# A second layout of the expert input's shift and scale: small products on TensorE, or a pass through DRAM

## What is computed

```python
mod = (jax.nn.silu(c) @ ada_w + ada_b)[:, None, :]
sh1, sc1, gt1, sh2, sc2, gt2 = jnp.split(mod, 6, axis=-1)
...
x = x + gt1 * (merged @ w_out)
h2 = rmsnorm(x, norm2_g) * (1.0 + sc2) + sh2
x = x + gt2 * hier_moe(h2, rg_w, rg_b, re_w, re_b, e_gate, e_up, e_down)
```

## Time and profile before

| | us |
|---|---|
| median of 3 runs | 2064.58 (2064.09 to 2065.99) |
| time of the profiled execution | 2064.39 |
| span of the profiled execution, first to last instruction | 2062.5 |
| PE busy in the span | 1926.4 |
| DVE busy | 1130.1 |
| ACT busy | 900.5 |

### The profile page before, as it was taken

How to read it: one execution, slowest core, us unless ns; L and a number is a source line. 1 busy time by engine, 2 the same in 40 slices (tenths; PEclk the granted TensorE clock), 3 DMA queues, 4 the chain that set the end, 5 groups by cost and what they waited for, 6 DMA issues and landing times.

```text
span 2062.5 us, 30821 instructions
## 1 busy us (share of the span) xinstructions
PE 1926.4 (93%) x12904; PEld 1493.4 (72%) x12904; DVE 1130.1 (55%) x1527; ACT 900.5 (44%) x1279; POOL 111.1 (5%) x91
## 2 busy tenths in 40 slices
PE   9999999999999876666699999999999999999998
PEld 7899988889984211111168888888888888988887
DVE  3778774577662110011146666756666766756666
ACT  4655455545352100000045556545455545675554
POOL 0244121001110000000000000000000000000000
PEclk9999999999999989898899999999999999999999
DMA  9654544678999999999986755544555555524552
GB/s 350 207 166 144 172 135 154 201 247 282 333 379 416 422 421 421 422 421 421 420 317 202 235 184 184 184 163 164 184 188 179 184 184 186 174 92 170 192 184 82
DMA packets 247505, 503.51 MB, mean 244 GB/s; under 512 B 12097, under 2 KB 166338, under 8 KB 223042
## 3 DMA queue, kind: packets, MB, share of 16 engines
q1 hardware_dynamic: 246464, 500.70, 67.5%
q10 hardware_dynamic: 898, 0.80, 0.1%
HBM read 500.07 MB, written 1.06 MB: 243 GB/s over the span
## 4 chain that ended last, share of the span: by engine, by line
PE 75%; DMA 12%; DVE 5%; SPq 3%; ACT 3%; issue 2%; POOL 0%; ACTq 0%; DVEq 0%
PE bank L600 14%; PE bank L602 14%; PE bank L601 14%; PE bank L661 13%; PE bank L663 7%; DMA m<-in_expert_w_up 5%; SPq L3298 3%; DMA m<-in_expert_w_down 3%; PE bank L1056 3%; DMA m<-in_expert_w_gate 2%; PE bank L1067 1%; PE bank L937 1%; DVE m L2225 1%; DMA m<-in_ffn_w_in 1%; ACT m L1532 1%
## 5 line engine op out<-in xcount | busy, mean ns | idle before, releaser
L2225 DVE TENSOR_TENSOR m<-m,m 128x1024 fp32r<-128x1024 f32 x505 | 623.0, 1248 | 281.2 <-ACT m L1532 279.0
L600 PE MATMUL bank<-m,m 128*128 128x256 f32 (+1 forms) x1960 | 662.3, 338 | 8.6 <-DVE m L2225 5.0
L602 PE MATMUL bank<-m,m 128*128 128x256 f32 (+1 forms) x1960 | 646.4, 330 | 0.0
L601 PE MATMUL bank<-m,m 128*128 128x256 f32 (+1 forms) x1960 | 646.3, 330 | 0.0
L1532 ACT ACTIVATE m<-m 128x1024 fp32r<-128x1024 f32 x505 | 523.7, 1054 | 219.7 <-PE bank L602 202.5
L661 PE MATMUL bank<-m,m 128*128 128x512 f32 x1248 | 439.8, 394 | 0.0
L600 PEld LDWEIGHTS bank<-m,m 128*128 128x128 f32 x1960 | 369.0, 188 | 58.6 <-DVE m L2225 11.5
L602 PEld LDWEIGHTS bank<-m,m 128*128 128x128 f32 x1960 | 369.1, 188 | 36.8
L601 PEld LDWEIGHTS bank<-m,m 128*128 128x128 f32 x1960 | 369.4, 188 | 35.4 <-issue 2.4
L663 PE MATMUL bank<-m,m 128*128 128x256 f32 x1248 | 353.0, 283 | 0.0
L661 PEld LDWEIGHTS bank<-m,m 128*128 128x128 f32 x1248 | 234.4, 188 | 53.7
(11 more groups left out here) (347 smaller groups left out, 1370.1 us busy)
## 6 DMA issues: line engine op xcount, KB each, us to landing
m<-in_ffn_w_in SPq DMA_DIRECT2D x88, 1024.0 KB, 5.1
m<-in_expert_w_up SPq DMA_DIRECT2D x64, 1024.0 KB, 26.4
m<-in_expert_w_gate SPq DMA_DIRECT2D x63, 1024.0 KB, 26.1
m<-in_w_in SPq DMA_DIRECT2D x60, 1024.0 KB, 5.2
m<-in_expert_w_down SPq DMA_DIRECT2D x60, 1024.0 KB, 26.1
m<-in_ffn_w_out SPq DMA_DIRECT2D x44, 1024.0 KB, 4.9
m<-in_ada_w SPq DMA_DIRECT2D x24, 1024.0 KB, 5.7
m<-in_a_w_in SPq DMA_DIRECT2D x16, 1024.0 KB, 5.3
```

The lines of the kernel that those rows point to most:

```text
L600: e.matmul(o, s[0], m[0], start=first, stop=False, skip_group_check=skip)
L601: e.matmul(o, s[0], m[1], start=False, stop=False, skip_group_check=skip)
L602: return e.matmul(o, s[1], m[0], start=False, stop=last, skip_group_check=skip)
L2225: inc(e.tensor_tensor(rv(fit(q.L, q.view.shape)), q.view, fit(q.H, q.view.shape), ALU.subtract), "l", skey(q, "L"))
```

## The change

The second set of products goes: PE no longer makes the `adap` sums, DVE no longer adds the bias to them, and `vp` shrinks to the gain `norm2_g` (one small load in place of three). Instead SP, in branch B step 1 behind the router's four small loads, writes the 16 finished columns of `cols` to the DRAM scratch, one number of 4 bytes at a time since neighbours on a partition lie 128 numbers apart in DRAM. In branch B step 2, behind the loads of that step's two products, SP waits for that write and reads the scratch back into `colp` in the other layout, 256 runs of 32 bytes.

```diff
-        vp, colp, g2p = tiny(24), tiny(16), tiny(8)
+        vp, colp, g2p = tiny(8), tiny(16), tiny(8)
...
                     full(ins, "ada", g)
-                    if g in (6, 7, 8, 9):
-                        b = take("s", "adap", g)
-                        half = 64 * (g % 2)
-                        for k in range(8):
-                            for r in (0, 32):
-                                ins = e.matmul(b[half + r:half + r + 32, 64 * k:64 * k + 4], acc[g][:, 8 * r + k:8 * r + 256:8],
-                                               K(C_ONE, 4), start=True, stop=True, skip_group_check=True)
-                        full(ins, "adap", g)
...
-                        if g in (6, 7, 8, 9):
-                            b = got("adap", g)
-                            w.wait_ge("vp")
-                            c, r = 8 * (kind - 3), slice(64 * half, 64 * half + 64)
-                            taken(e.tensor_tensor(colp[r, c:c + 8], b[r, 0:512:64], vp[r, c:c + 8], ALU.add), "adap", g,
-                                  also=[("colp", g)])
...
-                w.wait_ge("colp", 9)
-                inc(e.scalar_tensor_tensor(out=g2p, in0=colp[:, 8:16], scalar=1.0, in1=vp[:, 16:24], op0=ALU.add,
+                w.wait_ge("colp")
+                w.wait_ge("vp")
+                inc(e.scalar_tensor_tensor(out=g2p, in0=colp[:, 8:16], scalar=1.0, in1=vp, op0=ALU.add,
                                            op1=ALU.mult), "router", ("g2p",))
...
                     if name == "B" and i == 1:
                         w.wait_ge("full", ("ocT", 7))
                         router_in()
+                        w.wait_ge("aM")
+                        for g in range(6, 10):
+                            w.wait_ge("cols", g)
+                        then_inc(e.dma_start(bass.AP(tensor=scr, offset=0, ap=[[1, 128], [128, 16]]), cols[:, 16:32],
+                                             allow_slow_non_contiguous=True),
+                                 "scr_out", ("colq",), by=16)
+                    if name == "B" and i == 2:
+                        w.wait_ge("colq")
+                        in_rows = bass.AP(tensor=scr, offset=0, ap=[[8, 128], [1024, 2], [1, 8]])
+                        then_inc(e.dma_start(colp.rearrange("p (z k) -> p z k", z=2), in_rows), "skew_in", ("colp",), by=16)
...
-            for i, src in enumerate((a["ada_b"][0][3072:4096], a["ada_b"][0][4096:5120], a["norm2_g"][0])):
-                then_inc(e.dma_start(vp[:, 8 * i:8 * i + 8], src.rearrange("(p k) -> p k", k=8)), "vp_in", ("vp",), by=16)
+            then_inc(e.dma_start(vp, a["norm2_g"][0].rearrange("(p k) -> p k", k=8)), "vp_in", ("vp",), by=16)
```

## The result

The changed kernel takes **2068.49 us** (median of 20 runs, 2066.84 to 2070.26), the kernel before 2064.97 (20 runs beside them, 2063.78 to 2066.99). The ratio is 1.0017, with a 95% interval of 1.0011 to 1.0022: slower by 3.5 us, about 0.17%. The forecast was 2060.6 and the range ended at 2067.5. What came is near rival C, which had priced itself at 2068.1.

The account below looks back on a forecast made before the run. PE was taken to bound the product stages and to release the experts' DMA-bound stream. From the median 2064.58 us, -3.92 for PE and 0 for the rest, with the write's 3.0 us hidden, gave 2060.6; range 2059.4 to 2067.5.

Parts of the forecast that it names:

- rival C: DMA queue before branch C's first load: writes cost more than reads, 12.6 us, PE stalls 7.4, 2068.1 us; chance 0.15.
- The removed products: PE, groups 6 to 9: four places lose 0.98 us each, 3.92 us in all, passed on to the experts' stream.
- Rival D: From 505 to the experts: the DMA stream bounds, an earlier PE only waits longer, time near 2064.4; chance 0.04.
- The price of the write: SP's queue ahead of branch C's weight loads: 1.4 us issue plus 1.6 us packets, 3.0 us delay.
- the dear end of 7.0: Same write priced at full packets, 5.6 + 1.4 us: a PE stall of 1.8 us, gain shrinks to 2.1.
- The cover: Branch C's first weight load, landing at 508.98, may land as late as 514.1: 5.2 us of delay hidden.
- The sum: Whole kernel: -3.92 us for PE, 0 for the rest, giving 2060.6 us, 0.19% faster.
- estimate of 25.6 us for the write: The write, from the skill page's 0.2 us HBM latency: 128 accesses in turn on each engine, time near 2082.
- SP's wait and the read: SP, branch B step 2: write through at 505.8, 3.7 us left until 509.45, read 0.2 us; DVE does not wait.
- Rival E: Two early loads or freed banks give something, at most 2.08 us at the start: 2058.6 to 2059.8; chance 0.08.
- What would show it: Changed profile: no PE weight wait from 500 to 540 and `w_out` 3.9 us earlier confirm; a stall near 512 refutes.
- B: Branch C: the write costs 5.2 to 9.1 us, PE stalls, part of the gain lost, 2061.4 to 2064.5; chance 0.13.

Follow-up runs that it names:

- experiment 1: The changed kernel without the write to DRAM and the wait for it, the read kept: 2060.81 us, ratio 0.998 to the kernel before.
- (3): The changed kernel with the block transposed on PE and written as 16 rows of 512 B, whole computation: 2060.85 us, ratio 0.9981.
- twin read (2): The changed kernel with a read of the same 2048 4-byte pieces in the write's place, no second DMA: 2061.15 us, ratio 0.9983.
- 8: The changed kernel with the 2048 numbers written 64 bytes apart, whole computation: 2063.45 us, ratio 0.9991.
- 5: The changed kernel with 256 bytes between the written numbers, read back in two DMAs, whole computation: 2062.52 us, ratio 0.9991.
- (6): The changed kernel with only the eight shift columns written, 1024 pieces in place of 2048: 2066.72 us, ratio 1.0009.
- (4): The changed kernel with 20 idle 128 x 128 products on PE ahead of branch C's first wait: 2066.12 us, ratio 1.0005.

## Why the prediction was wrong, point by point

- **The removed products: right.** 4 x 0.98 = 3.92 us forecast. Branch B starts 4.23 us earlier (0.21 of it is there before the first of the four places, 386.60 - 386.39), and without the write (1) or with cheap rows (3) the kernel is 4.2 us faster, so the gain is passed on to the end, as claimed. Rival D falls.
- **The price of the write: the step that failed.** "I lean to the low half, since the nearest rows in size and place are the router's small packets." The rows were reads, and the twin read (2) shows that they price a read well: about 1 us. The write delays the load behind it by 10.9 us instead of the 3.0 taken, and the dear end of 7.0 did not hold it either. A price per packet was the wrong form: with a distance of 64 or 256 bytes as many writes cost 3.4 and 2.5 us (8, 5), and half as many neighbours cost 8.3 (6).
- **The cover: right in size.** 5.2 us were counted. The delay of 10.9 us, less 5.2, would be a stall of 5.7; PE's wait is 5.91.
- **Left out: the clock.** After that wait the granted clock is 0.50, the 1.2 GHz level, and PE starts the 18 products from 518.70 to 522.50 at 0.21 us apart (from the second on) where 0.12 is usual. The Trainium skill, "TensorE: Matmul & The Clock Gate", section "Wait — 56ns, not 53.3ns?", gives a start-to-start of the columns over 1.2 GHz at this level, by which an estimate for 256 columns is 213 ns; the rows agree (0.21 us). What it cost is read from the rows: the distance to the kernel before grows from 2.36 us at 518.70 to 3.76 at 522.64, 1.40 us. With PE kept busy (4) the clock does not fall. The distance grows by another 0.37 us until 555.04, at a clock of 1.00, as products start 0.120 us apart where it was 0.119; from 526 to 546 they do so in experiment 1 as well, which has no stall, so this is not the price of the write. Its cause is open.
- **The sum, mended.** At line 694 PE is 4.11 us ahead. From there to branch C's first product it takes 518.70 - 511.77 = 6.93 us, where it took 516.34 - 515.88 = 0.46: 6.47 more. -4.11 + 6.47 + 1.40 + 0.37 = +4.13 us, as the profiled spans differ (4.1); the medians differ by 3.5.
- **Rival C: right in direction and place, not in its form; its time is in part luck.** It said a small write costs the memory more than a small read, in the queue ahead of branch C's first load, with a stall of 7.4 and 2068.1 us. The direction is what the twin read (2) shows. But it counted per packet, its delay was 12.6 us where 10.9 came, and it had no term for the clock: one miss makes up for the other. The prediction's estimate of 25.6 us for the write is more than twice what was measured. The page it cited, "DMA: Bandwidth & Descriptors" of the Trainium skill, warns of a read-modify-write below 512 bytes; all 2048 pieces are below it in experiments 5 and 8 too, where the delay is a quarter to a third, so the rule warns of such writes and does not give the size.
- **SP's wait and the read: no cost, as forecast, but not the times.** The read is held until 511.96, by the two loads ahead of it, and its issue holds SP for another 4.20 us, so the next `ada_w` load goes out at 516.21 (509.45 before). PE does not feel it: the distance stays at 4.13 us. The operation that needs the read runs at 540.17, 17.7 us after it lands (511.96 + 10.5). Rival E: nothing seen beyond 0.3 us.
- **What would show it.** The prediction named a stall near 512 with ACT waiting for a weight load as the sign of B or C, and that is what stands there. Its other sign, that the write takes the DMA engines more than about 5 us, came too. It also said that the packets would tell the price, and they did not: nearly all end in time, and the bytes after them are missing.

Shown by removal, by direction, by distance and by queue: writes of 4 bytes to neighbouring addresses bring the DMA engines down to 0 to 68 GB/s for 8 to 9 us, whichever queue issues them. Open: what happens inside the memory or the engines, whether it matters that several engines write the neighbours, how far apart is far enough, why columns 32 KB apart double it, and why the landing varies between 14.8 and 17.1 us. Each layout was profiled once, so small differences of landings say nothing.

## What to carry to other kernels

Price a scattered write to DRAM neither from reads of the same size nor per piece: ask whether neighbouring addresses are written in pieces of their own, and if so turn the block on chip first, so that each row goes out whole (16 rows of 512 B: no cost that can be measured, against 7.7 us). Look for its price in the GB/s of the microseconds behind it and in the landing of the loads on every queue, not in the times of its own packets. And when a stall of several microseconds on PE is in a sum, add what the products behind it cost at the lower clock.

## What the runs showed of the hardware that was not expected

- Nearly all of 2048 writes of 4 bytes have a recorded end within some 3 us, and then the engines move 0 to 53 GB/s until 511; the same happens when they are issued from another queue (0 to 68 GB/s from 489 to 497).
- The landing of the load behind them, by the layout of the writes: 6.0 us (rows of 512 B), 7.3 (read instead), 8.7 (256 B apart), 9.6 (64 B apart), 14.5 (half of the neighbours), 17.1 (all neighbours), 32.2 (neighbours, columns 32 KB apart).
- Columns 32 KB apart cost 2.5 us of delay when the numbers within them are 256 B apart (5) and are the worst case when they are dense (9).
- Adding 40 idle matmuls of 4.6 us went with a kernel 2.4 us faster: PE's clock stayed at 1.00, and the load landed earlier in that profile.
